# A two-layer hybrid trunk on one core: exponents and low parts as steps of their own, other PSUM banks for the token groups

## The chip, the cores and the metric

One core of a Trainium2 chip. The metric is the device time of one execution in microseconds; the time before is the median of three runs. All matrix work is in fp32 or in a split of fp32 in two parts, on TensorE (PE); the other engines are VectorE (DVE), ScalarE (ACT), GpSimd (POOL) and SyncE (SP), which issues the DMAs.

## What is computed

A trunk of two layers on 512 tokens of width 1024. The parts around the change are the attention with sinks and the retention of each layer:

```python
for l in range(DEPTH):
    h = rms_norm(x, norm_mix_g[l])
    aq, ak, av, rq, rk, rv, rg, sz, sxbc, sdt = jnp.split(h @ w_in[l], offs, axis=-1)
    ya = swa_sink_attention(aq, ak, av, attn_sinks[l], attn_bias)
    yr = retention(rq, rk, rv, rg, ret_gn_g[l])
    ys = ssd_mixer(sz, sxbc, sdt, ...)
    x = x + jnp.concatenate([ya, yr, ys], axis=-1) @ w_out[l]
    h = rms_norm(x, norm_ffn_g[l])
    x = x + conv_ffn(h, ffn_w_up[l], ...)
return rms_norm(x, final_norm_g)
# attention: chunks of 64 queries, 128 keys, 8 heads
p = softmax(concat([logits + bias, sink]))[..., :-1];  out = p @ v
# retention: q, k rotated; per head y normed by its mean and variance, scaled, times silu(g)
```

## The kernel before

**Split weights.** Every product of the dense parts is three matmuls of 128x512: w_hi with h_hi, w_hi with h_lo, and w_lo with h_hi. The weights stream through four slots. A pack is 128 by 512 (four tiles of 128x128): SP loads it into `w_raw` once POOL has made the low part of the pack before it in the slot, ScalarE copies it rounded into `w_hi` (L516) once PE has finished the run that used the slot (`run_done`), and POOL subtracts to get `w_lo` (L405). ScalarE makes packs where its own program says so: `hi_to(p)` makes all up to p, and each waits for its slot. A unit of eight tiles is 24 matmuls, of four tiles 12.

**The order.** All five engines follow one list of names by hand, `SCHEDULE` (L91), for the part of a layer up to the output projection. Each engine runs its own share of a step, in the order of the list, and passes over a step that has no share for it. A wait stands in the program of the engine that waits, so whatever comes later in the list on that engine stands behind it. The steps that matter here:

- `GQ0..3`, `GV0..3`: the first four packs of the token groups (retention's q and k; its v). PE works on all four blocks of 128 tokens at once, one PSUM bank for each token block, `token_banks`/`group_banks` = dense0, dense1, mix2, mix3 (L793, L1162). `LQ0..3`, `LV0..3`: the last four packs, one token block after the other. On DVE, `LQn` is the rotation and `LVn` the centring of a block (L1010 to L1012, evacuating the bank). On ScalarE, `LQ3` and `LV3` make four packs; `LV3` the ones for D20 and D21, whose slots LV3 itself frees.
- `ASn`: logits of two chunks on PE in banks mix0 and mix1, and transposed v in mix4; DVE adds the bias, takes the maximum and the sink's difference (L951 to L967); ScalarE copies the v window (L623) and takes the exponents, one of the sinks and eight of 128x128 (L626, L629).
- `AXn`: DVE divides by the sum (L971 to L974). `ATn`: PE transposes the probabilities into mix2 and mix3, ScalarE copies them (L634). `AVn`: PE's product with v, ScalarE's high part (L640), DVE's low part (L984).
- `Dn`: dense unit n, on bank n % 2; PE waits until unit n - 2 is evacuated, DVE evacuates (L836, or L827 for the output projection, D28 to D51, where x is added). D20 to D23 are the gate z of the SSD, D24 to D27 that of the retention; ScalarE applies silu to them (L564, L569).
- `ZMn`: DVE multiplies by silu(z) (L843), ScalarE squares (L610); after ZM1 and ZM3 POOL adds two squares (L437), and `SN0`, `SN1` sum over partitions on PE; ScalarE makes the factor, `SXn` scales (L937) and splits two tiles (L533 on ScalarE, L774 on DVE).
- `RXn`: retention's output tile, scaled and gated on DVE (L1049, L1051), high part on ScalarE, low part on DVE (L1054), which waits for ScalarE in between. D44 to D51 read these tiles, D44 waiting for each one as it comes to it.

SB, SA, RT, RA, RB and the like are steps of the SSD and of the retention that the change doesn't touch. After the list come the gated MLP's two halves: loops over 12 and 10 pairs of up units (`up(0)`, `up(1)`), each half followed by eight down units.

`unit()` (L1114) runs a unit. With `wait_for_tile` it waits, tile by tile, for the activations: D44 (`ret_tile`), the first down unit of each half (`g_tile`, L1463) and `up(0)` of the first half (`h_tile`, L1135, where the normed x of tile 7 comes last).

Of the kernel before, what the change touches and what calls it, by code (L numbers as in the profile page):

```python
# [19 lines left out]
D, S, P = 1024, 512, 128  # L20
# [5 lines left out]
NB = S // BLK  # L26
# [5 lines left out]
SLOTS = 4  # L32
# [6 lines left out]
GROUP = 4  # L39
# [18 lines left out]
def segments():  # L58
# [31 lines left out]

SCHEDULE = (  # L91
# [5 lines left out]
).split()  # L97


# [94 lines left out]
def build(nc, a, out):  # L194
    f32, f32r = mybir.dt.float32, mybir.dt.float32r
    ALU, ACT, AX = mybir.AluOpType, mybir.ActivationFunctionType, mybir.AxisListType
    with ExitStack() as ctx:
# [247 lines left out]
        def _(act):  # L445
# [60 lines left out]
            with act.Fori(0, DEPTH) as l:  # L506
# [28 lines left out]
                for name in SCHEDULE:  # L535
# [85 lines left out]
                    elif step == "AS":  # L621
                        act.wait_ge(m_ready[4], ready(name, 2, l))
                        nc.scalar.activation(vwin[:, n % 2, :, :], M[4][:, 0:2 * P].rearrange(  # L623
                            "p (c d) -> p c d", c=2), ACT.Copy).then_inc(m_free[4], 1)
                        act.wait_ge(lg_in, l * 4 + n + 1)
                        link(nc.scalar.activation(sk[:, :], sk[:, :], ACT.Exp))  # L626
                        for r in range(8):
# [80 lines left out]
        def _(dve):  # L708
# [58 lines left out]
            with dve.Fori(0, DEPTH) as l:  # L767
# [22 lines left out]
                            link(ins)  # L790
                    ins.then_inc(conv_summed, 1)

                token_banks = (dense[0], dense[1], M[2], M[3])  # L793
                V.memset(ak[:, 0:CH], 0.0)
                V.memset(av[:, 0:CH], 0.0)
                for name in SCHEDULE:
# [179 lines left out]
                    elif step == "AV":  # L976
                        av_bank = banks_of(name)[0]
                        for c in range(2):
# [3 lines left out]
                            if c == 0:  # L982
# [1 line left out]
                            V.tensor_tensor(m_lo[:, 4:8, at:at + CH], src,  # L984
                                            m_hi[:, 4:8, at:at + CH].bitcast(f32), ALU.subtract)\
                                .then_inc(m_free[av_bank] if c else a_lo, 1)
                    elif step == "LQ":
                        if n:
                            dve.wait_ge(rot_done, l * 4 + n)
                        dve.wait_ge(run_done, l * N_SEGS + (SEG0 + UNIT_END[U_RK + n]))  # L990
# [11 lines left out]
                                               ALU.mult, ALU.mult).then_inc(evac, 1)  # L1002
                        dve.wait_ge(evac, l * N_EV + U_RK + n + 1)
                        V.tensor_tensor(qk[:, n, :], qk[:, n, :], rot[:, :], ALU.add).then_inc(rot_done, 1)
                    elif step == "LV":
                        if n:
                            dve.wait_ge(evac, l * N_EV + U_RV + n)
                        dve.wait_ge(run_done, l * N_SEGS + (SEG0 + UNIT_END[U_RV + n]))
# [6 lines left out]
                    elif step == "RA":  # L1015
                        dec = consts["decin"][:, :].rearrange("p (t j s) -> p t j s", t=2, j=2)
                        for j in range(2):
                            dve.wait_ge(m_ready[1 + j], ready(name, j, l))
                            V.tensor_tensor(ar("rpt", 2, 2)[:, :, j, :], M[1 + j][:, 0:256].rearrange(
                                "p (t s) -> p t s", t=2), dec[:, :, j, :], ALU.mult).then_inc(m_free[1 + j], 1)  # L1020
                        V.tensor_tensor(kd.rearrange("p (h d) -> p h d", h=4),
                                        qk[:, n, 0:256].rearrange("p (h d) -> p h d", h=4),
                                        consts["kdec"][:, :].unsqueeze(2).broadcast_to([P, 4, 64]), ALU.mult)
                        V.tensor_tensor(qd, qkt[:, n % 2, 2:4, :],
                                        consts["qdec"][:, :].rearrange("p (t s) -> p t s", t=2),
                                        ALU.mult).then_inc(qd_done, 1)
                    elif step == "RB":
                        if n < NB - 1:
                            dve.wait_ge(m_ready[5], ready(name, 2, l))
                            if n == 0:  # L1030
                                V.tensor_copy(rst, M[5][:, 0:256].rearrange("p (t s) -> p t s", t=2))\
                                    .then_inc(m_free[5], 1)
                            else:
                                for t in range(2):
                                    ins = V.scalar_tensor_tensor(rst[:, t, :], rst[:, t, :],
                                                                 consts["gch"][:, t:t + 1],
                                                                 M[5][:, P * t:P * t + P], ALU.mult, ALU.add)
                                    if t == 0:
                                        link(ins)
                                ins.then_inc(m_free[5], 1)  # L1040
                    elif step == "RQ":
                        c = slice(BLK * n, BLK * n + BLK)
                        dve.wait_ge(r_sqh, l * NB + n + 1)
                        V.tensor_tensor(m_lo[:, 8:12, c], rsq[:, :, c], m_hi[:, 8:12, c].bitcast(f32),
                                        ALU.subtract).then_inc(r_sql, 1)
                    elif step == "RX":
                        dve.wait_ge(r_rs, l * 4 + n + 1)
                        dve.wait_ge(g_silu, l * 4 + n + 1)
                        link(V.scalar_tensor_tensor(ry[:, n, :], ry[:, n, :], par["gng"][:, bass.ds(l * 4 + n, 1)],  # L1049
                                                    rs4[n], ALU.mult, ALU.mult))  # L1050
                        V.tensor_tensor(ry[:, n, :], ry[:, n, :], sg[:, n, :], ALU.mult).then_inc(rn_done, 1)  # L1051
                        dve.wait_ge(r_hi, l * 4 + n + 1)
                        dve.wait_ge(rn_done, l * 4 + n + 1)
                        lo_from(m_lo[:, 8 + n, :], ry[:, n, :], m_hi[:, 8 + n, :], r_lo)  # L1054
# [47 lines left out]
        def _(pe):  # L1102
# [8 lines left out]
            mm(dense[1][0:8, 0:8], relw, relw).then_inc(run_done, SEG0)  # L1111
            pe.wait_ge(relt_ready, 1)

            def unit(bankno, number, runs, src_hi, src_lo, wait_for_tile=None):  # L1114

                pe.wait_ge(evac, number + 1)
                d = dense[bankno][:, :]
                last = runs[-1][3] + runs[-1][4] - 1
                for slot, pack, t0, k0, m in runs:
                    pe.wait_ge(hi_ready, pack + 1)  # L1120
                    for j in range(m):
                        w = w_hi[:, slot, P * (t0 + j):P * (t0 + j) + P]
# [30 lines left out]
            def take(name, i, l):  # L1153

                pe.wait_ge(m_free[banks_of(name)[i]], ready(name, i, l))

            with pe.Fori(0, DEPTH) as l:
                def dense_unit(n, src, wait_for_tile=None):
                    runs = [(p % SLOTS, l * N_PACKS + p, t0, k0, m) for p, t0, k0, m in SEGS[n]]
                    unit(n % 2, l * N_EV + n - 2, runs, *src, wait_for_tile)  # L1160

                group_banks = (dense[0], dense[1], M[2], M[3])  # L1162

                def group_mm(u, k, low, start=False, stop=False):
# [41 lines left out]
                def token_mm(t, k, low, start=False, stop=False):  # L1206

                    w = (w_lo if low else w_hi)[:, k % SLOTS, :]
                    c = slice(BLK * t, BLK * t + BLK)
                    d = group_banks[t][:, :]  # L1210
                    ins = mm(d, h_hi[:, k, c], w, start, stop)
                    return ins if low else mm(d, h_lo[:, k, c], w, False, False)

                def token_pack(u, k):

                    pe.wait_ge(hi_ready, l * N_PACKS + 2 * u + k + 1)
                    for t in range(NB):
                        if k == 0 and u == U_RK and t >= 2:
                            take("AT0", t - 2, l)
                        elif k == 0:  # L1220
                            pe.wait_ge(evac, l * N_EV + u + t + 1 - (2 if u == U_RK else GROUP))
                        token_mm(t, k, False, start=k == 0)
                    pe.wait_ge(lo_ready, l * N_PACKS + 2 * u + k + 1 + SLOTS)
                    for t in range(NB):
# [22 lines left out]
                for name in SCHEDULE:  # L1247
# [132 lines left out]
                    elif step == "AT":  # L1380
                        pe.wait_ge(p_done, l * 4 + n + 1)
                        if n == 0:
                            pe.wait_ge(evac, l * N_EV + U_RV + NB)
                        l4 = lg.rearrange("p (g c m k) -> p g c m k", g=2, c=2, m=2)
                        for c in range(2):
                            take(name, c, l)
# [246 lines left out]
```

## Time and profile before

| | us |
|---|---|
| median of three runs | 1294.49 (1293.77 to 1294.52) |
| profiled execution | 1293.96 |
| its span, first to last instruction | 1292.2 |
| PE busy | 1263.6 (98%) |
| DVE, ACT, POOL busy | 627.6, 580.9, 585.0 |
| mean granted TensorE clock | 0.996 of full |

How to read it: matmuls overlap, one of 128x512 lasts 0.39 us and the next starts 0.227 us behind it, so a time on PE is best read from start to start. The names are the kernel's tiles (`dense`, `mix` are PSUM; `arena` is a shared SBUF area that holds most mixer tiles). Layer 0 has its attention at 118 to 205 us, layer 1 at 753 to 840.

### The profile page before, as it was taken

The page shows a single profiled execution, that of the slowest core. Times are in us where ns is not written, and L with a number is a line of the kernel's source. Part 1 is how long each engine was busy: PE and PEld are TensorE (multiplying, and loading weights), DVE is VectorE, ACT ScalarE, POOL GpSimd, SP SyncE. Part 2 cuts the span into 40 slices and gives each one's busy share as a digit, 9 for nine tenths or more (in the row PEclk, how much of TensorE's full clock was granted, in tenths as well). Part 3 has the DMA queues.
Part 4 walks back from the last instruction along what each step waited for, and adds up shares of the span by engine and source line. Part 5 has one row for each costly group of instructions (what it writes and reads, how often), then busy time and mean ns, then how long its engine had stood idle before and what let it go on. Part 6 is the DMA issues. An engine that isn't in the chain of part 4 may idle for free.

```text
span 1292.2 us, 21140 instructions
## 1 busy us (share of the span) xinstructions
PE 1263.6 (98%) x6066; PEld 1025.8 (79%) x6066; DVE 627.6 (49%) x962; ACT 580.9 (45%) x966; POOL 585.0 (45%) x438
## 2 busy tenths in 40 slices
PE   8999899999999999999999999999999999999996
PEld 5887678788888888888878877787888888888885
DVE  5858565564544103332248686545754430133323
ACT  6443395555443224443345236854643432244433
POOL 4543333355444445554445333425354444455541
PEclk9999999999999999999999999999999999999998
DMA  6353222243333333333333622213233333333333
GB/s 213 104 149 89 66 66 66 65 115 98 96 94 95 98 98 92 97 96 98 99 83 84 171 66 82 73 51 99 74 114 97 97 98 98 90 97 97 97 94 111
DMA packets 77483, 124.89 MB, mean 97 GB/s; under 512 B 7752, under 2 KB 20456, under 8 KB 77416
## 3 DMA queue, kind: packets, MB, share of 16 engines
q1 hardware_dynamic: 77416, 124.03, 33.8%
q8 instruction: 38, 0.62, 0.2%
q14 instruction: 29, 0.24, 0.1%
HBM read 121.45 MB, written 2.55 MB: 96 GB/s over the span
## 4 chain that ended last, share of the span: by engine, by line
issue 39%; PE 34%; POOL 18%; ACT 3%; DVE 3%; POOLq 2%; DMA 0%; SPq 0%; DVEq 0%; ACTq 0%
PE dense L1106 32%; POOL w_lo L405 18%; PE mix L1106 2%; POOLq L404 1%; DVE h_lo L735 1%; POOLq L418 1%; DMA x<-in_xT 0%; ACT w_hi L516 0%; DVE arena L1097 0%; DVE arena L1049 0%; ACT m_hi L533 0%; ACT arena L629 0%; ACT h_hi L458 0%; DVE x L827 0%; DVE ssq L743 0%
## 5 line engine op out<-in xcount | busy, mean ns | idle before, releaser
L405 POOL TENSOR_TENSOR w_lo<-w_raw,w_hi 128x512 fp32r<-128x512 f32 x424 | 576.5, 1374 | 676.3 <-ACT w_hi L516 670.5
L1106 PE MATMUL dense<-h_hi,w_hi 128*128 128x512 f32 x992 | 391.3, 394 | 3.8 <-DVE h_lo L735 3.1
L1106 PE MATMUL dense<-h_lo,w_hi 128*128 128x512 f32 x992 | 387.0, 390 | 0.0
L516 ACT ACTIVATE w_hi<-w_raw 128x512 fp32r<-128x512 f32 x422 | 256.6, 626 | 285.0 <-PE dense L1106 227.9
L1106 PE MATMUL dense<-h_hi,w_lo 128*128 128x512 f32 x992 | 266.4, 390 | 0.0
L1106 PEld LDWEIGHTS dense<-h_hi,w_hi 128*128 128x128 f32 x992 | 186.6, 188 | 46.1 <-issue 6.6
L1106 PEld LDWEIGHTS dense<-h_hi,w_lo 128*128 128x128 f32 x992 | 186.4, 188 | 40.5 <-issue 1.7
L1106 PEld LDWEIGHTS dense<-h_lo,w_hi 128*128 128x128 f32 x992 | 186.7, 188 | 39.5 <-issue 1.4
L1106 PE MATMUL dense<-m_hi,w_hi 128*128 128x512 f32 x544 | 213.4, 392 | 1.3 <-DVE x L827 1.3
L1106 PE MATMUL dense<-m_lo,w_hi 128*128 128x512 f32 x544 | 212.0, 390 | 0.0
L1106 PE MATMUL dense<-m_hi,w_lo 128*128 128x512 f32 x544 | 146.8, 389 | 0.0
L1106 PEld LDWEIGHTS dense<-m_hi,w_hi 128*128 128x128 f32 x544 | 102.1, 188 | 24.2 <-DVE x L827 3.0
L1106 PEld LDWEIGHTS dense<-m_hi,w_lo 128*128 128x128 f32 x544 | 102.1, 188 | 21.3
L1106 PEld LDWEIGHTS dense<-m_lo,w_hi 128*128 128x128 f32 x544 | 102.2, 188 | 20.9
L1087 DVE TENSOR_TENSOR x<-dense,x 128x512 f32<-128x512 f32 x32 | 22.1, 692 | 191.4 <-PE dense L1106 191.4
L1065 DVE TENSOR_TENSOR arena<-dense,rstd 128x512 f32<-128x512 f32 x44 | 30.4, 692 | 87.1 <-PE dense L1106 87.1
L687 ACT ACTIVATE arena<-arena 128x512 f32<-128x512 f32 x44 | 27.8, 632 | 85.7 <-DVE arena L1072 85.7
L1075 DVE TENSOR_TENSOR arena<-dense,rstd 128x512 f32<-128x512 f32 x44 | 30.4, 691 | 71.4 <-PE dense L1106 71.4
L1068 DVE SCALAR_TENSOR_TENSOR arena<-arena,params 128x512 f32<-128x512 f32 x44 | 35.5, 807 | 59.8 <-ACT arena L682 59.8
L458 ACT ACTIVATE h_hi<-x,params 128x512 fp32r<-128x512 f32 x39 | 28.2, 723 | 71.1 <-DVE x L1087 59.6
L827 DVE TENSOR_TENSOR x<-dense,x 128x512 f32<-128x512 f32 x48 | 32.6, 687 | 54.3 <-PE dense L1106 54.3
L1106 PE MATMUL mix<-arena 64*128 64x128 f32 (+4 forms) x696 | 57.2, 301 | 1.6 <-ACT arena L634 1.6
(203 smaller groups left out, 1191.4 us busy)
## 6 DMA issues: line engine op xcount, KB each, us to landing
w_raw<-in_w SPq DMA_DIRECT2D x428, 256.0 KB, 2.6
arena<-cum_rows SPq DMA_DIRECT2D x8, 512.0 KB, 6.1
x<-in_xT SPq DMA_DIRECT2D x8, 256.0 KB, 5.7
out_y<-arena SPq DMA_DIRECT2D x8, 256.0 KB, 2.2
arena<-exp_rows SPq DMA_DIRECT2D x12, 128.0 KB, 6.5
consts<-in_consts SPq DMA_DIRECT2D x1, 839.0 KB, 7.6
rel_scratch<-arena SPq DMA_DIRECT2D x1, 382.0 KB
bias<-rel_scratch SPq DMA_DIRECT2D x8, 32.0 KB, 2.4
```

Of the source, the lines that this page charges most:

```text
L404: pool.wait_ge(hi_ready, pack + 1)
L405: nc.gpsimd.tensor_tensor(w_lo[:, s, :], w_raw[:, s, :], w_hi[:, s, :].bitcast(f32), ALU.subtract).then_inc(lo_ready, 1)
L418: with pool.Fori(g0, g1) as i:
L458: nc.scalar.activation(h_hi[:, o, :], x[:, o, :], ACT.Copy, scale=gcol(e, o)).then_inc(h_hi_ready, 1)
L516: nc.scalar.activation(w_hi[:, slot, :], w_raw[:, slot, :], ACT.Copy).then_inc(hi_ready, 1)
L687: nc.scalar.activation(fs, fy, ACT.Silu).then_inc(f_silu, 1)
L827: V.tensor_tensor(x[:, o, :], d[:, :], x[:, o, :], ALU.add).then_inc(evac, 1)
L1065: V.tensor_tensor(fpad[:, 2:2 + S], dense[0][:, :], rstd[:, :], ALU.mult).then_inc(evac, 1)
L1068: ins = V.scalar_tensor_tensor(fy, fpad[:, 1:1 + S], par["fconv"][:, bass.ds(fi * 4 + 1, 1)], fy, ALU.mult, ALU.add)
L1075: V.tensor_tensor(fb, dense[1][:, :], rstd[:, :], ALU.mult).then_inc(evac, 1)
L1087: V.tensor_tensor(x[:, o, :], dense[n % 2][:, :], x[:, o, :], ALU.add).then_inc(evac, 1)
L1106: return T.matmul(dst, lhsT, rhs, start=start, stop=stop)
```

## The change

The list is rewritten: `QE` and `VE` are now DVE's evacuations of the token groups, `AE` the exponents on ScalarE, `RL` the low part of RX on DVE. `LQ`, `LV`, `AS` and `RX` keep the rest. In the list, AE0 stands behind GV3 and SB3; AT0 and AS1 stand ahead of LV3, and VE3 behind AS1; AX1 stands ahead of AV0, and ZM0 behind D21; AT2 stands ahead of SX0 and ZM3; each RL stands one D step behind its RX. The token groups' first two blocks take mix2 and mix3, the last two dense0 and dense1, with the waits that follow from it. In units with `wait_for_tile`, the last run is made by `last_run`, which takes the low parts of the weights of all tiles but the last before it waits for the last tile.

```diff
@@ SCHEDULE
-    "GQ0 GQ1 GQ2 GQ3 SB1 SA2 LQ0 LQ1 LQ2 LQ3 SB2 SA3 GV0 GV1 AS0 GV2 GV3 SB3 AX0 LV0 LV1 LV2 LV3 AT0 AS1 "
-    "D20 AV0 AX1 ZM0 D21 ZM1 AT1 AS2 D22 AX2 AV1 SN0 ZM2 D23 SX0 ZM3 AT2 AS3 D24 AX3 AV2 SN1 D25 SX1 D26 AT3 D27 AV3 "
+    "GQ0 GQ1 GQ2 GQ3 SB1 SA2 LQ0 QE0 LQ1 QE1 LQ2 QE2 LQ3 QE3 SB2 SA3 GV0 GV1 AS0 GV2 GV3 SB3 AE0 AX0 "
+    "LV0 VE0 LV1 VE1 LV2 VE2 AT0 AS1 LV3 AE1 VE3 D20 AX1 AV0 D21 ZM0 ZM1 AT1 AS2 AE2 D22 AX2 AV1 SN0 ZM2 "
+    "D23 AT2 SX0 ZM3 AS3 AE3 D24 AX3 AV2 SN1 D25 SX1 D26 AT3 D27 AV3 "
...
-    "D35 RX0 D36 RX1 D37 D38 RX2 D39 RX3 D40 D41 D42 D43 D44 D45 D46 D47 D48 D49 D50 D51"
+    "D35 RX0 D36 RL0 RX1 D37 RL1 D38 RX2 D39 RL2 RX3 D40 RL3 D41 D42 D43 D44 D45 D46 D47 D48 D49 D50 D51"
@@ ScalarE, step AS
                             "p (c d) -> p c d", c=2), ACT.Copy).then_inc(m_free[4], 1)
+                    elif step == "AE":
                         act.wait_ge(lg_in, l * 4 + n + 1)
@@ VectorE
-                token_banks = (dense[0], dense[1], M[2], M[3])
+                token_banks = (M[2], M[3], dense[0], dense[1])
...
-                    elif step == "LQ":
+                    elif step == "QE":
...
-                    elif step == "LV":
+                    elif step == "VE":
...
                         V.tensor_tensor(ry[:, n, :], ry[:, n, :], sg[:, n, :], ALU.mult).then_inc(rn_done, 1)
+                    elif step == "RL":
                         dve.wait_ge(r_hi, l * 4 + n + 1)
@@ TensorE
+            def last_run(d, run, src_hi, src_lo, wait_for_tile):
+                slot, pack, t0, k0, m = run
+                pe.wait_ge(hi_ready, pack + 1)
+                hi = [w_hi[:, slot, P * (t0 + j):P * (t0 + j) + P] for j in range(m)]
+                lo = [w_lo[:, slot, P * (t0 + j):P * (t0 + j) + P] for j in range(m)]
+                for j in range(m - 1):
+                    wait_for_tile(k0 + j)
+                    mm(d, hi[j], src_hi(k0 + j), start=k0 + j == 0, stop=False)
+                    mm(d, hi[j], src_lo(k0 + j), start=False, stop=False)
+                pe.wait_ge(lo_ready, pack + 1 + SLOTS)
+                for j in range(m - 1):
+                    mm(d, lo[j], src_hi(k0 + j), start=False, stop=False)
+                wait_for_tile(k0 + m - 1)
+                mm(d, hi[-1], src_hi(k0 + m - 1), start=False, stop=False)
+                mm(d, lo[-1], src_hi(k0 + m - 1), start=False, stop=False)
+                mm(d, hi[-1], src_lo(k0 + m - 1), start=False, stop=True).then_inc(run_done, 1)
@@ unit()
                 for slot, pack, t0, k0, m in runs:
+                    if wait_for_tile is not None and k0 + m - 1 == last and m > 1:
+                        last_run(d, runs[-1], src_hi, src_lo, wait_for_tile)
+                        continue
@@ token_mm, token_pack
-                    d = group_banks[t][:, :]
+                    d = token_banks[t][:, :]
...
-                        if k == 0 and u == U_RK and t >= 2:
-                            take("AT0", t - 2, l)
+                        if k == 0 and u == U_RK and t < 2:
+                            take("AT0", t, l)
                         elif k == 0:
-                            pe.wait_ge(evac, l * N_EV + u + t + 1 - (2 if u == U_RK else GROUP))
+                            pe.wait_ge(evac, l * N_EV + u + t + 1 - GROUP)
@@ TensorE, step AT
                         if n == 0:
-                            pe.wait_ge(evac, l * N_EV + U_RV + NB)
+                            pe.wait_ge(evac, l * N_EV + U_RV + 2)
```

## Rows read from the trace of the kernel before

**Rows 1.** The page's busy us, share of the span and instructions, PE.
```profile
PE 1263.6 (98%) x6066; PEld 1025.8 (79%) x6066; DVE 627.6 (49%) x962; ACT 580.9 (45%) x966; POOL 585.0 (45%) x438
```
**Rows 2.** PE's waits in the whole span: line, releaser, us in total, times, longest.
```profile
PE mix L1390 <- DVE arena L1012: 4.2, 2, 2.1
...
PE mix L1106 <- ACT arena L634: 1.6, 2, 0.8
...
PE dense L1106 <- POOL w_lo L405: 1.3, 2, 0.7
...
PE dense L1106 <- DVE x L827: 1.3, 4, 0.4
```
**Rows 3.** Windows from start to start: length, each engine's busy us, PEclk, DMA.
```profile
98.78:101.61 2.83, 2.83 (x15) 2.35 (x14) 2.83 (x11) 0.00 (x0) 0.00 (x0) 1.00 0.56 161
126.53:131.04 4.51, 3.48 (x16) 2.12 (x13) 4.29 (x8) 2.05 (x6) 2.52 (x2) 1.00 0.10 15
139.22:141.48 2.26, 0.17 (x2) 0.01 (x1) 1.93 (x3) 0.78 (x2) 2.26 (x3) 1.00 0.38 82
141.48:145.39 3.91, 3.91 (x26) 3.46 (x27) 0.01 (x1) 1.19 (x2) 1.57 (x2) 0.56 0.71 212
157.67:158.59 0.92, 0.16 (x1) 0.00 (x0) 0.92 (x2) 0.00 (x0) 0.00 (x0) 1.00 0.00 0
158.59:160.90 2.31, 2.31 (x26) 2.02 (x27) 1.15 (x2) 1.72 (x4) 0.50 (x1) 1.00 0.04 7
181.83:182.78 0.95, 0.16 (x1) 0.00 (x0) 0.95 (x2) 0.95 (x3) 0.45 (x1) 1.00 0.14 54
244.96:250.95 5.99, 5.77 (x25) 4.43 (x24) 5.22 (x7) 1.68 (x3) 2.54 (x2) 1.00 0.17 44
253.67:259.83 6.16, 5.75 (x26) 4.43 (x24) 3.11 (x5) 2.72 (x5) 3.64 (x3) 1.00 0.29 85
267.00:272.44 5.44, 5.44 (x26) 4.50 (x25) 2.89 (x5) 3.79 (x8) 3.10 (x3) 1.00 0.32 80
284.31:290.27 5.96, 5.70 (x25) 4.43 (x24) 4.72 (x8) 3.16 (x4) 1.30 (x1) 1.00 0.35 88
776.82:779.12 2.30, 2.30 (x26) 2.02 (x27) 0.01 (x1) 1.09 (x2) 1.58 (x2) 1.00 0.63 181
```
**Rows 4.** Order in time, SB3 to VE0 and AX1's multiply: start, us, instruction.
```profile
124.91 1.69 PE L1106 MATMUL mix<-arena 128*64 128x128 f32 x32
...
125.09 2.45 ACT L629 ACTIVATE arena<-arena,nmx 128x128 f32<-128x128 f32 x8
...
127.44 1.14 ACT L516 ACTIVATE w_hi<-w_raw 128x512 fp32r<-128x512 f32 x2
...
128.13 2.52 POOL L405 TENSOR_TENSOR w_lo<-w_raw,w_hi 128x512 fp32r<-128x512 f32 x2 [4.66 <-ACT w_hi L516]
...
129.71 2.02 DVE L974 TENSOR_TENSOR arena<-arena,den 128x1024 f32<-128x1024 f32 x1
...
131.65 0.68 DVE L1010 TENSOR_REDUCE vmean<-dense 128x4 f32<-128x512 f32 x1
...
132.63 0.75 DVE L1012 SCALAR_TENSOR_TENSOR arena<-dense,rstdc,vmean 128x512 f32<-128x512 f32 x1
...
157.31 1.22 DVE L974 TENSOR_TENSOR arena<-arena,den 128x1024 f32<-128x1024 f32 x1
```
**Rows 5.** Order in time, the silu of D21, then AT2's copies, ZM's sum, SN1.
```profile
160.75 0.62 ACT L564 ACTIVATE pad<-pad 128x512 f32<-128x512 f32 x1
...
182.15 1.07 ACT L634 ACTIVATE arena<-mix 128x512 f32<-128x512 f32 x2
...
182.33 1.28 POOL L437 TENSOR_TENSOR sq<-sq 128x512 f32<-128x512 f32 x1 [2.73 <-ACT sq L610]
...
183.86 1.13 PE L1106 MATMUL mix<-sq,consts 128*128 128x512 f32 x2
```
**Rows 6.** Order in time, one low part in the up loop.
```profile
400.86 1.30 POOL L405 TENSOR_TENSOR w_lo<-w_raw,w_hi 128x512 fp32r<-128x512 f32 x1 [0.78 <-ACT w_hi L516]
```

More of the change, by code:

```diff
@@ L1160, in dense_unit @@
                     unit(n % 2, l * N_EV + n - 2, runs, *src, wait_for_tile)
+                token_banks = (M[2], M[3], dense[0], dense[1])
                 group_banks = (dense[0], dense[1], M[2], M[3])
```

## The prediction

> **What bounds the kernel now.** I read the page's busy shares first: TensorE (PE) is busy 98% of the span [rows 1], so only PE's gaps and slow stretches can pay. An unhindered unit of 24 matmuls of 128x512 takes 5.44 us, 0.227 each [rows 3], and the change adds and removes no matmul. What PE waits for is the second view [rows 2]: 4.2 us, once per layer, for VectorE's evacuation of the retention values (L1012), and 1.3 to 1.6 us each for ScalarE's copies of the probabilities (L634), POOL's low parts (L405) and the evacuation of x (L827). The third view is windows cut at instruction starts [rows 3]; a window less the same work unhindered is what its wait costs, the slow restart with it. The fourth is the order in time around the first softmax and around the second group norm [rows 4, 5].
>
> **The change, part by part, per layer.**
>
> *Exponents as a step AE, behind GV3.* Now ScalarE runs the eight exponents from 125.09 to 127.54 and only then converts the last two packs of the value group, though their slots are free when GV2 and GV3 end, the latter before SB3's start at 124.91 and the former one pack (12 x 0.227 = 2.7 us) sooner; POOL's low parts follow at 128.13 [rows 4], and PE stands in LV0 twice. LV0 takes 4.51 us [rows 3]; twelve matmuls behind mixer work take 2.83. With both conversions ahead (1.14 / 2 = 0.57 each, a low part 2.52 / 2 = 1.26) the last high part is there at 125.6 and the last low part at 127.0; LV0 starts at 126.53 and asks for the low parts from 128.4 on. Gain 4.51 - 2.83 = 1.68. Price: the exponents start behind the last conversion and end at 125.6 + 0.2 (the sinks') + 2.45 = 128.27, which is 0.73 later.
>
> *Token banks.* AT0 needs the two mixer banks. Now tokens 2 and 3 sit there and AT0 waits for all four evacuations: PE stands 2.26 us (139.22 to 141.48) [rows 3]. Then tokens 0 and 1 are there, AT0 and AS1 go ahead of LV3, and AT0 asks for VE1 at the end of LV2: 126.53 + 2.83 + 2 x 2.72 = 134.80. The vector side: the division AX0 now ends at 131.65, 4.11 us behind the exponents [rows 4]. Its last multiply took 2.02 us beside POOL's low parts (busy 128.13 to 130.65), and the same multiply 1.22 us at 157.31 [rows 4]. In the new order POOL has nothing from 127.0 until LV3, so I take 1.22: AX0 ends at 128.27 + 4.11 - 0.80 = 131.58, an evacuation takes 1.73 (131.65 to the end of L1012, 133.38), VE0 and VE1 end at 135.05. That is 0.25 behind PE; as the small add of that chain was slowed too, I take 0.2. Gain 2.26 - 0.2 = 2.06. With 2.02 instead, AT0 waits 1.05 and the gain is 1.2. The Trainium skill ("SBUF — State Buffer", section "SBUF: two separate sides") says the port pair that VectorE and GpSimd share is an exclusive lock, taken by a two-input vector instruction or a GpSimd one for its whole length; by that rule the multiply is short where POOL is idle, which gives the first price, while a machine on which the 2.02 had another cause would give the second, 1.7 us more for the kernel.
>
> *The clock.* In layer 0 the granted clock reads 0.56 (near 1.2 of 2.4 GHz) for 141.48 to 145.39, right behind that stand; AT0 with AS1 takes 3.91 us there and 2.31 for AT1 with AS2 at full clock. In layer 1 an equal stand is followed by 2.30 at clock 1.00 [rows 3]. So 1.60 us comes back, once, in layer 0. Bounds: 0, if another wait draws the clock down, and 1.6.
>
> *LV3 behind AS1.* LV3, 2.72 us, now covers AS1's vector work; its own evacuation VE3 stands behind AS1's vector part (like kinds of instructions as AX0, so at most its 4.1 us) and ends by 137.1 + 4.1 + 1.73 = 142.9. D21 alone waits for it, at about 146.6 (D20 from 140.1, 5.44, AV0 about 1.1); D20 waits for VE2 only. ScalarE's four conversions for D20 and D21 now queue behind AT0's two copies (1.07 [rows 5]) and AS1's window copy, whose PE work ends before LV3 starts; LV3 frees the first slot 0.7 later. Cost nothing. If that cover goes, D20 waits up to 0.6 for one conversion.
>
> *Division AX1 ahead of AV0's low part, ZM0 behind D21.* Now AX1's multiply ends at 157.31 + 1.22 = 158.53 and AT1, having stood 0.92 us, starts at 158.59 [rows 3, 4]. New: the exponents end at about 140.0 + 0.6 + 0.2 + 2.45 = 143.3, D20's evacuation by 146.3, AX1 takes at most 4.1 and is done by 150.4; D21 ends at 152.1. Gain 0.92. AV0's low part is asked for by D36 only.
>
> *AT2 ahead of SX0 and ZM3 on ScalarE.* AV2 stands 0.95 us for AT2's copies [rows 2, 3]. They now come before SX0's splits, so this wait goes. But SN1 follows AV2 directly and waits for POOL's sum of ZM2 and ZM3, ready at 183.61, with SN1 started at 183.86 [rows 5]: that chain runs silu of D23, SX0's high parts, their low parts on VectorE, ZM3, square, sum, and the copies, 1.07 us, are put in front of it. Against that ScalarE gets ahead: the silu of D21 ran 0.15 before D22's start (160.75 against 160.90), since ZM0's square stood before it; with ZM0 behind D21 it can run 1.4 before, and this stretch is ScalarE's queue throughout, so I carry 1.2 through. SN1 can start 1.2 - 1.07 = 0.13 sooner by the chain, plus 0.2 for the slack it had: gain 0.3. Bounds: 0.95 (chain covers nothing) and a loss of 0.8 (nothing of the 1.2 arrives).
>
> *RX split into RX and RL.* Now VectorE sits through ScalarE's split before each low part, x is evacuated late, and D39 and D42 wait. The pairs D38 with D39 and D41 with D42 take 5.99 and 6.16 us against 5.44 [rows 3]. New, each RX costs VectorE two instructions and RL one, with a unit's work between a split and its low part. At 0.75 for the scaled kind and 0.68 for a plain one [rows 4], four RX and RL and five evacuations are 4 x (0.75 + 0.68 + 0.68) + 5 x 0.68 = 11.8 us, in five units of PE, 13.6, and an evacuation has a whole unit before it is missed. Some of these run slower beside POOL, as the division's multiply did, so I keep half of the gain as a bound: 0.55 + 0.72 = 1.27, from 0.6. RL3 is done four units before D44's last tile.
>
> *last_run.* In the first up unit PE stands for the last tile's low part; 5.96 against 5.44 [rows 3]. Three low matmuls (0.68 us) now go ahead of that tile, more than the 0.52: gain 0.5. D44, the first down units and the other up(0) iterations show no such wait: 0. The wait for the packs' low parts moves 0.45 us earlier. The code issues as many instructions; no DMA is added or moved, SP's and POOL's queues keep their order.
>
> **The sum.** 1.68 + 2.06 + 0.92 + 0.3 + 1.27 + 0.5 = 6.73 per layer, 13.5 for two; with the clock's 1.6, 15.1 us. The profiled execution took 1293.96 (span 1292.2, 1.8 around it): 1278.9. The median of the three runs, 1294.49, is 0.5 above it: **1279.4**.
>
> **Rivals.**
> *A: AT0 still waits, for AX0.* Multiply at 2.02, or the later exponents pushing more. For: the margin is under 0.3. Against: POOL has no work then. 1.7 us of gain less, and if a remaining stand of over 2 us kept the clock low, 1.6 more: 1281 to 1283.
> *B: SN1 becomes the wait.* The copies stretch a chain that was ready 0.25 ahead of PE. For: ScalarE has little idle time there. Against: the earlier silu. 2 x (0.3 + 0.8) = 2.2 less: 1281.6. With A: 1283.5.
> *C: slower.* The wait for low parts, hoisted in last_run, passes 30 times (24 up units, 6 others). It decides if low parts arrive later than asked: to turn 15.1 us into a loss of 2.6 each pass must cost 0.59 us. Against: in the up loop a low part made at 400.86 to 402.16 [rows 6] is asked for at 409.5 in the new order, 7.3 us of slack. It would give 1297.
> *D: nothing moves*: the waits only change their names, each gain taken by the next wait in the same layer. It needs every cover above to be false. 1294.5.
>
> **Chances.** Forecast 0.72 (own range 1277.5 to 1281), A or B or both 0.24, C 0.02, D 0.02. Range: the forecast's, widened to A and B and to the clock's bound: 1276.8 to 1283.5. A measurement of this kernel tells apart about 0.2% (2.6 us). Faster 0.96, same 0.02, slower 0.02.
>
> **What would show it.** Right: LV0 near 2.8 us with no wait on L516 or L405; the wait on L1012 under 0.5; clock 1.00 through AT0; AT1 with no wait on L974; AV2 with none on L634, and SN1 with one on POOL L437 of 0.5 to 0.8; no waits on x (L827) at D39 and D42; the first up unit at 5.44. Wrong: a stand at AT0 over 1 us (A), SN1 later than 23 us behind D22's start (B), waits on POOL's low parts inside the up loop (C), or a new wait of D20 or D21.

## The result, and the profile after

The changed kernel takes 1279.45 us, the median of four runs (1279.37 to 1279.6), against 1294.13 for the kernel before in the same comparison (1292.02 to 1294.52). The ratio is 0.989, with a 95% interval of 0.9873 to 0.9907. The forecast was 1279.4. The profiled execution took 1279.5, with a span of 1277.6: 14.6 less than before.

That the total fits does not make every term right. The page first, where PE's share answers to [rows 1]:

```profile
PE 1257.4 (98%) x6066; PEld 1025.3 (80%) x6066; DVE 630.5 (49%) x962; ACT 581.9 (46%) x966; POOL 586.5 (46%) x438
```

PE's longest waits over the whole span (line, releaser, total, times, longest), which answer to [rows 2]. The changed kernel's lines lie lower in the file: L405 is now L406, L634 is L636, L827 is L829, L1012 is L1014, L1106 is L1109 and L1390 is L1415:

```profile
PE dense L1109 <- DMA arena<-in_rel: 3.4, 1, 3.4
PE dense L1109 <- DVE h_lo L737: 2.6, 1, 2.6
PE mix L1109 <- POOL sq L438: 2.6, 2, 1.3
```

All four waits of [rows 2] have gone. The first two belong to the kernel's start. One is new: 1.3 us per layer for POOL's sum of squares (L438), ahead of SN1.

Windows from start to start in layer 0, in the columns of [rows 3]. They are LV0; AT0 with AS1; AT1 with AS2; AV2 up to SN1; D38 with D39; D41 with D42; the first up unit:

```profile
126.25:129.10 2.85, 2.85 (x16) 2.36 (x13) 2.25 (x5) 1.69 (x6) 0.47 (x1) 1.00 0.59 170
134.54:136.79 2.25, 2.25 (x27) 1.96 (x27) 1.68 (x4) 1.09 (x2) 0.00 (x0) 1.00 0.00 0
151.80:154.05 2.25, 2.25 (x28) 1.96 (x26) 1.96 (x3) 1.86 (x3) 1.35 (x1) 1.00 0.47 117
175.06:177.43 2.37, 1.09 (x10) 0.50 (x9) 2.27 (x4) 2.09 (x3) 1.26 (x1) 1.00 0.00 0
238.55:243.99 5.44, 5.44 (x25) 4.51 (x24) 4.23 (x6) 1.68 (x3) 2.55 (x2) 1.00 0.16 48
246.71:252.17 5.46, 5.46 (x25) 4.50 (x24) 3.17 (x5) 2.72 (x5) 2.98 (x3) 1.00 0.26 62
276.65:282.10 5.45, 5.45 (x25) 4.50 (x24) 4.72 (x8) 3.16 (x4) 1.29 (x1) 1.00 0.33 96
```

The number behind the length is PE's busy time; it equals the length in every row but the fourth. There PE is busy 1.09 of 2.37 us. AV2 itself took 1.08 before, from 182.78 [rows 3] to 183.86 [rows 5], so SN1 now stands 1.29 (a stand is the time that PE waits ahead of a step).

The order in time (start, us, instruction) around the first softmax, from D21 to the exponents of AE2, from the silu of D23 to SN1, and layer 1's first product after its norm:

```profile
125.49 2.45 ACT L631 ACTIVATE arena<-arena,nmx 128x128 f32<-128x128 f32 x8
...
129.67 1.22 DVE L976 TENSOR_TENSOR arena<-arena,den 128x1024 f32<-128x1024 f32 x1
...
133.66 0.75 DVE L1014 SCALAR_TENSOR_TENSOR arena<-mix,rstdc,vmean 128x512 f32<-128x512 f32 x1
...
134.54 1.03 PE L1415 MATMUL mix<-consts,arena 128*128 128x128 f32 x8
...
152.60 2.37 DVE L845 TENSOR_TENSOR arena<-arena,pad 128x512 f32<-128x512 f32 x2
...
152.70 1.72 POOL L406 TENSOR_TENSOR w_lo<-w_raw,w_hi 128x512 fp32r<-128x512 f32 x1 [1.43 <-ACT w_hi L517]
...
152.72 0.63 ACT L565 ACTIVATE pad<-pad 128x512 f32<-128x512 f32 x1
...
154.90 1.27 DVE L953 SCALAR_TENSOR_TENSOR arena<-mix,bias 128x512 f32<-128x512 f32 x2
...
158.44 2.45 ACT L631 ACTIVATE arena<-arena,nmx 128x128 f32<-128x128 f32 x8
...
171.24 0.63 ACT L565 ACTIVATE pad<-pad 128x512 f32<-128x512 f32 x1
...
171.77 1.07 ACT L636 ACTIVATE arena<-mix 128x512 f32<-128x512 f32 x2
...
172.73 1.15 ACT L534 ACTIVATE m_hi<-arena 128x512 fp32r<-128x512 f32 x2
...
176.03 1.26 POOL L438 TENSOR_TENSOR sq<-sq 128x512 f32<-128x512 f32 x1 [3.69 <-ACT sq L611]
...
177.43 1.12 PE L1109 MATMUL mix<-sq,consts 128*128 128x512 f32 x2 [1.28 <-POOL sq L438]
...
652.67 1.92 PE L1109 MATMUL mix<-x,wdt_g 128*32 128x512 f32 x16
```

The division's multiply beside an idle POOL takes 1.22 (it was 2.02 [rows 4]). VE1 ends at 133.66 + 0.75 = 134.41, and AT0 starts at 134.54, when PE gets to it. The copies of AT2 (171.77) do stand ahead of SX0's high parts (172.73), and POOL's sum, the end of that chain, comes 1.29 after PE wants it.

Cutting both traces at the same instruction, the product with `wdt_g`, gives a second measure that run-to-run noise at the kernel's ends doesn't touch. From layer 0's to layer 1's it was 25.53 to 660.89 before, 635.36 us, and is 25.27 to 652.67 now, 627.40. So layer 0 gained 7.96, layer 1 gained 6.34 (from this cut to the last sum of squares 617.61 and 611.27), and the start 0.26, which sum to 14.56. Below, "the layer" is this length in layer 0; 627.40 is what it is held against.

### The profile page after: what moved, and what is told of

Its sections match the earlier page's. It is cut to its first block, busy times and chain, and to the rows that moved or that the text cites. A ratio compares the mean times of both kernels' runs of the same rounds, so it can differ in the third digit from the quotient of the medians.

```text
span 1277.6 us, 21142 instructions
## 1 busy us (share of the span) xinstructions
PE 1257.4 (98%) x6066; PEld 1025.3 (80%) x6066; DVE 630.5 (49%) x962; ACT 581.9 (46%) x966; POOL 586.5 (46%) x438
## 4 chain that ended last, share of the span: by engine, by line
PE 41%; issue 38%; POOL 18%; POOLq 2%; DVE 1%; ACT 1%; DMA 0%; SPq 0%; DVEq 0%; ACTq 0%
PE dense L1109 38%; POOL w_lo L406 18%; PE mix L1109 2%; POOLq L405 1%; POOLq L419 1%; DVE ssq L761 0%; DVE arena L1100 0%; DMA x<-in_xT 0%; DVE ssq L745 0%; ACT h_hi L459 0%; PE mix L1432 0%; POOL sq L438 0%; ACT L481 0%; ACT L478 0%; DVE ones_r L768 0%
## 5 line engine op out<-in xcount | busy, mean ns | idle before, releaser
L406 POOL TENSOR_TENSOR w_lo<-w_raw,w_hi 128x512 fp32r<-128x512 f32 x424 | 577.9, 1377 | 655.6 <-ACT w_hi L517 651.0
L1109 PE MATMUL dense<-h_hi,w_hi 128*128 128x512 f32 x992 | 390.7, 394 | 2.9 <-DVE h_lo L737 2.6
L1109 PE MATMUL dense<-h_lo,w_hi 128*128 128x512 f32 x992 | 386.7, 390 | 0.0
L1109 PE MATMUL dense<-h_hi,w_lo 128*128 128x512 f32 x992 | 270.1, 390 | 0.0
L1109 PEld LDWEIGHTS dense<-h_hi,w_hi 128*128 128x128 f32 x992 | 186.5, 188 | 44.2 <-issue 4.3
L1109 PEld LDWEIGHTS dense<-h_hi,w_lo 128*128 128x128 f32 x992 | 186.3, 188 | 40.5 <-issue 1.7
L1109 PEld LDWEIGHTS dense<-h_lo,w_hi 128*128 128x128 f32 x992 | 186.6, 188 | 39.6 <-issue 1.4
L1109 PE MATMUL dense<-m_hi,w_hi 128*128 128x512 f32 x544 | 212.9, 391 | 0.0
L1109 PE MATMUL dense<-m_lo,w_hi 128*128 128x512 f32 x544 | 211.8, 389 | 0.0
L1109 PE MATMUL dense<-m_hi,w_lo 128*128 128x512 f32 x544 | 147.7, 389 | 0.0
L1109 PEld LDWEIGHTS dense<-m_hi,w_hi 128*128 128x128 f32 x544 | 102.1, 188 | 21.3
L1109 PEld LDWEIGHTS dense<-m_hi,w_lo 128*128 128x128 f32 x544 | 102.1, 188 | 21.3
L1109 PEld LDWEIGHTS dense<-m_lo,w_hi 128*128 128x128 f32 x544 | 102.2, 188 | 21.0
L829 DVE TENSOR_TENSOR x<-dense,x 128x512 f32<-128x512 f32 x48 | 33.0, 688 | 56.5 <-PE dense L1109 56.3
L1109 PE MATMUL mix<-arena 64*128 64x128 f32 (+4 forms) x696 | 56.3, 297 | 0.0
```

What stands on the lines that cost most here:

```text
L406: nc.gpsimd.tensor_tensor(w_lo[:, s, :], w_raw[:, s, :], w_hi[:, s, :].bitcast(f32), ALU.subtract).then_inc(lo_ready, 1)
L829: V.tensor_tensor(x[:, o, :], d[:, :], x[:, o, :], ALU.add).then_inc(evac, 1)
L1109: return T.matmul(dst, lhsT, rhs, start=start, stop=stop)
```

## The experiments

Each is the changed kernel with one edit, unless two are named. The kernel before, run beside them, had medians of 1293.8 to 1293.9; the changed kernel was not timed again beside them. So where two medians differ by about 1 us or less, the layer's length has to show the same. Expectations stand as they were on record before the run.

**AT2 back behind ZM3.**

```diff
-    "D23 AT2 SX0 ZM3 AS3 AE3 D24 ...
+    "D23 SX0 ZM3 AT2 AS3 AE3 D24 ...
```

> The changed kernel with one part undone: AT2 behind SX0 and ZM3 again. Theory (the copies were put into the chain that SN1 waits for, so the move bought nothing): AV2 stands about 1 us for the copies again, and SN1 then starts with no stand, about 0.3 us sooner than now (1.28 us of stand on POOL L438 in each layer now); the kernel 0 to 0.6 us faster than the changed one, 1278.9 to 1279.5. Rival (the move is worth the 0.95 us stand it removed): about 0.9 per layer slower, 1281.3.

Measured: 1277.75 (1277.67 to 1277.96), ratio 0.9872 [0.9855, 0.9888], layer 626.52. This part of the change makes the kernel 1.7 us slower, where the prediction's term had it 0.6 faster (2 x 0.3). The time is 1.2 below the expected range, since AV2 stands half of the 1 us that was expected. The order in time of this kernel:

```profile
171.14 0.63 ACT L565 ACTIVATE pad<-pad 128x512 f32<-128x512 f32 x1
...
171.68 1.14 ACT L534 ACTIVATE m_hi<-arena 128x512 fp32r<-128x512 f32 x2
...
174.79 1.07 ACT L636 ACTIVATE arena<-mix 128x512 f32<-128x512 f32 x2
...
174.97 1.28 POOL L438 TENSOR_TENSOR sq<-sq 128x512 f32<-128x512 f32 x1 [2.72 <-ACT sq L611]
...
175.43 1.14 PE L1109 MATMUL mix<-arena 128*64 128x256 f32 x8 [0.39 <-ACT arena L636]
```

POOL's sum starts at 174.97 against 176.03, 1.06 sooner; 0.10 of this is the silu's, the rest comes of the copies (1.07), which are no longer in its way. SN1's stand is gone, and AV2 waits 0.39 for the copies. It starts 1.46 behind the start of D24's last four matmuls (173.97), against 0.99 in the changed kernel, so PE loses 0.47 here instead of the 1.29 at SN1.

**ZM0 back ahead of D21's silu.**

```diff
-    "... D20 AX1 AV0 D21 ZM0 ZM1 AT1 ...
+    "... D20 AX1 AV0 ZM0 D21 ZM1 AT1 ...
```

> The changed kernel with ZM0 ahead of D21 again (D20 AX1 AV0 ZM0 D21 ZM1). The prediction took ZM0's move to bring ScalarE's queue 1.2 us forward up to SN1; the changed kernel's trace shows only about 0.5. Theory: ZM0 ahead of D21 can run in VectorE's idle time while D21 is on PE, so that ZM1 comes sooner, and SN1's stand (1.28) gets no longer or even shorter by up to 0.7 per layer: 1278.0 to 1279.5. Rival (the prediction's): the move is worth about 1.2 to the chain, and undone SN1 stands up to 2.5: 1281.9.

Measured: 1278.65 (1278.53 to 1278.72), ratio 0.9885 [0.9869, 0.9902], layer 626.97. The theory held. Its order in time (the line at 154.01 is D22's start), and its wait at SN1:

```profile
149.34 0.69 DVE L845 TENSOR_TENSOR arena<-arena,pad 128x512 f32<-128x512 f32 x1
...
152.68 0.63 ACT L565 ACTIVATE pad<-pad 128x512 f32<-128x512 f32 x1
...
153.35 1.14 DVE L845 TENSOR_TENSOR arena<-arena,pad 128x512 f32<-128x512 f32 x1 [0.70 <-ACT pad L565]
...
154.01 0.48 PE L1109 MATMUL dense<-h_hi,w_hi 128*128 128x512 f32 x1
...
157.95 2.45 ACT L631 ACTIVATE arena<-arena,nmx 128x128 f32<-128x128 f32 x8
```

```profile
PE mix L1109 <- POOL sq L438: 1.7, 2, 0.8
```

One multiply runs early and alone in 0.69; the changed kernel runs both in a row beside POOL's low part, 2.37 for the two. AE2's exponents come at 157.95 instead of 158.44, and SN1's stand falls from 1.3 to 0.8. And the silu of D21 runs 154.01 - 152.68 = 1.33 ahead of D22 here, exactly as in the changed kernel (152.72 and 154.05). So moving ZM0, which was to let ScalarE get ahead, won nothing on ScalarE; it only put two multiplies in a row on VectorE, which costs 0.43 in the layer and 0.8 us for the kernel.

**Both of these together.** The edits are the two above.

> The changed kernel with AT2 behind ZM3 and ZM0 ahead of D21, the two orders of before that each made it faster when put back alone (1277.75 and 1278.65). Theory: AT2 behind ZM3 leaves AV2 a stand of 0.55 us for the copies, ScalarE's queue comes 0.45 sooner with ZM0 in VectorE's idle time, so AV2 stands 0.1 and SN1 not at all: 0.45 per layer below 1277.75, 1276.9. Rival (the two act on the same wait and the second buys nothing): 1277.7.

Measured: 1276.64 (1276.32 to 1276.91), ratio 0.9867 [0.985, 0.9883], layer 626.11. It beats both kernels. PE's only waits in its trace are both at the kernel's start; none of the mixers' is left:

```profile
PE dense L1109 <- DMA arena<-in_rel: 3.3, 1, 3.3
PE dense L1109 <- DVE h_lo L737: 2.6, 1, 2.6
```

The layer is 627.40 - 626.11 = 1.29 shorter, SN1's whole stand.

**ZM3 ahead of SX0, AT2 where the change put it.** This shortens the chain to SN1 from the other side.

```diff
-    "D23 AT2 SX0 ZM3 AS3 AE3 D24 ...
+    "D23 AT2 ZM3 SX0 AS3 AE3 D24 ...
```

> The changed kernel with ZM3 ahead of SX0 (D23 AT2 ZM3 SX0 AS3). Theory: SX0's two splits and two low parts leave the chain to POOL's sum (about 2 us of it), the sum is ready some 1.3 us before AV2 ends, SN1 stands for nothing; two layers of 1.28 us: 1276.9. Rival: ScalarE and VectorE are full there, so AS3, AX3 or SX1 come late instead and the stand only moves: 1278.5 to 1279.5.

Measured: 1280.52 (1280.16 to 1280.83), ratio 0.9892 [0.9876, 0.9909], layer 627.86. The forecast of 1276.9 missed. The rival beside it had the mechanism, a stand that only moves, but this time is 1.0 above its range too. Its waits on PE, and two lines in order of time:

```profile
PE dense L1109 <- ACT w_hi L517: 1.7, 2, 0.9
...
PE mix L1109 <- ACT arena L636: 0.7, 2, 0.3
```

```profile
173.80 1.63 POOL L438 TENSOR_TENSOR sq<-sq 128x512 f32<-128x512 f32 x1 [1.41 <-ACT sq L611]
...
174.32 2.27 DVE L776 TENSOR_TENSOR m_lo<-arena,m_hi 128x512 fp32r<-128x512 f32 x2
```

SN1 no longer waits, but SX0's low parts now run beside POOL's sum and take 2.27 for the two, and ScalarE's queue is late by D27: 0.9 us for a high part there and 0.3 at AV3. The wait was passed on.

**SN1 behind D25.**

```diff
-    "... D24 AX3 AV2 SN1 D25 SX1 D26 AT3 ...
+    "... D24 AX3 AV2 D25 SN1 SX1 D26 AT3 ...
```

> The changed kernel with SN1 behind D25 instead of behind AV2. Theory: PE has D25's 5.4 us to do while POOL's sum is made, SN1's stand of 1.28 goes, and the group norm comes 4 us later on ScalarE, which has little idle time there: as with ZM3 ahead of SX0, part of it returns as waits for conversions at D27 or for the copies at AV3 or for SX1's low parts at D28: 1277 to 1279.5. Rival (that queue has slack enough): 1276.8.

Measured: 1283.17 (1281.12 to 1285.27), ratio 0.9923 [0.9906, 0.9939], layer 628.55. A miss. Its wait, at AV3:

```profile
PE mix L1109 <- ACT arena L636: 4.7, 2, 2.3
```

I had counted what PE gains by taking a dense unit first. The scale factor, SX1's splits and, behind them, AT3's copies all stand behind SN1's sum, so they came later (the copies start at 195.60), and AV3 stood 2.3 us. That is beyond the range of 1277 to 1279.5, which allowed for a part of it.

**AX1 back behind AV0's low part.**

```diff
-    "... D20 AX1 AV0 D21 ZM0 ZM1 AT1 ...
+    "... D20 AV0 AX1 D21 ZM0 ZM1 AT1 ...
```

> The changed kernel with AX1 behind AV0's low part again (D20 AV0 AX1 D21), ZM0 left behind D21. Theory: VectorE waits about 3 us for ScalarE's high part (table load, silu, two splits) before it divides, AT1 stands 0.9 us per layer again: 1281.3. Rival (the stand before was ZM0's or another wait of PE, and AX1 is early enough now): no stand at AT1, 1279.5.

Measured: 1280.38 (1279.5 to 1281.05), ratio 0.9897 [0.988, 0.9913], layer 627.61. It lies between the theory (1281.3) and the rival (1279.5), and neither had the reason. Its waits in the mixers:

```profile
PE mix L1415 <- DVE arena L976: 1.8, 2, 0.9
...
PE mix L1109 <- POOL sq L438: 0.7, 2, 0.4
```

The stand of 0.9 at AT1 came back, yet the layer is only 0.2 longer (the median is 0.9 above, but in this profile the product with `wdt_g` came at 26.18 instead of 25.27, before any of the edit): the chain of VectorE and ScalarE behind it runs on, so PE comes later to a sum that is ready when it was, and SN1's stand falls from 1.3 to 0.4. The profiled execution (1280.82) is 1.3 above the changed kernel's: 0.9 of it lies ahead of the edit, and 0.4, two layers of 0.2, are the edit's. The silu of D21, with AX1 back and ZM0 left behind D21, starts at 154.35, 1.73 ahead of D22 (156.08).

**The same edit where SN1 doesn't wait,** with AT2 behind ZM3.

> The changed kernel with AT2 behind ZM3 and AX1 behind AV0's low part. With SN1's stand there, putting AX1 back cost only about 0.2 us per layer, as AT1's 1.05 of stand was taken off SN1's. Theory (one slack, shared): without SN1's stand only AV2's 0.55 is left to take it from, so AX1's place is now worth 1.05 - 0.55 = 0.5 per layer: 1278.7. Rival (AX1's place is worth little in itself, as VectorE catches up anyway): as u_at2, 1277.8 to 1278.1.

Measured: 1279.22 (1279.12 to 1280.13), ratio 0.9889 [0.9873, 0.9906], layer 627.18. AX1's place is worth 1279.22 - 1277.75 = 1.5 us here, 627.18 - 626.52 = 0.66 in the layer, against 0.2 in the layer above. The only wait beside those of the start:

```profile
PE mix L1415 <- DVE arena L976: 1.8, 2, 0.9
```

The mechanism is the one of the theory (one slack, shared), the size 0.5 us above its 1278.7. AT1's stand replaced AV2's (0.47 in the kernel without this edit), just as it took most of SN1's above. These gains lie one behind the other on the same slack and don't add.

**Exponents back ahead of the last conversions.**

```diff
-    "... GV0 GV1 AS0 GV2 GV3 SB3 AE0 AX0 "
+    "... GV0 GV1 AS0 AE0 GV2 GV3 SB3 AX0 "
```

> The changed kernel with AE0 back right behind AS0, ahead of the conversions of GV2 and GV3. Theory: LV0 takes 4.5 us again (waits on L517 and L406), AX0's multiply runs beside POOL's low parts and takes 2.0 us again, and since LV0 is later by 1.7, AT0 still has no stand: 3.4 us slower than the changed kernel, 1282.8. Rival (conversions were hidden by the later exponents' own price, AT0's wait for AX0): under 1.5 slower, below 1281.

Measured: 1282.9 (1282.37 to 1283.09), ratio 0.991 [0.9893, 0.9926], layer 629.12. As expected. PE's longest wait in LV0, then POOL and VectorE in order of time:

```profile
PE mix L1109 <- POOL w_lo L406: 1.3, 2, 0.7
```

```profile
128.04 2.52 POOL L406 TENSOR_TENSOR w_lo<-w_raw,w_hi 128x512 fp32r<-128x512 f32 x2 [4.66 <-ACT w_hi L517]
...
128.84 0.51 DVE L974 TENSOR_TENSOR den<-den,sk 128x8 f32<-128x8 f32 x1
...
129.62 2.02 DVE L976 TENSOR_TENSOR arena<-arena,den 128x1024 f32<-128x1024 f32 x1
```

The multiply takes 2.02 again, now that POOL works beside it, and the small add of 128x8 ahead of it 0.51, where the changed kernel has 0.17 (at 129.23). The two kernels differ in AE0's place alone.

**The old banks and the old place of LV3.** AT0 waits for all four evacuations again, and the waits of the token packs follow the banks as they did before; the steps' split stays.

```diff
-                token_banks = (M[2], M[3], dense[0], dense[1])
+                token_banks = (dense[0], dense[1], M[2], M[3])
...
-    "LV0 VE0 LV1 VE1 LV2 VE2 AT0 AS1 LV3 AE1 VE3 D20 ...
+    "LV0 VE0 LV1 VE1 LV2 VE2 LV3 VE3 AT0 AS1 AE1 D20 ...
...
-                            pe.wait_ge(evac, l * N_EV + U_RV + 2)
+                            pe.wait_ge(evac, l * N_EV + U_RV + NB)
```

> The changed kernel with the token banks as before (dense0, dense1, mix2, mix3), LV3 and VE3 ahead of AT0, and AT0 waiting for all four evacuations. Theory: AT0 stands 2.2 us in each layer (4.4 us), and where the stand is followed by a granted clock near half, as in layer 0 before, 1.6 more: 1283.9 without and 1285.5 with one such stretch. Rival (the banks matter little once AE0 is moved): under 2 us slower, below 1281.5.

Measured: 1286.18 (1285.31 to 1287.3), ratio 0.9935 [0.9918, 0.9952], layer 631.25. It is the dearest part, 6.7 us. Windows of the profiled run: the stand, then AT0 with AS1 and what follows in layer 0, and the same two in layer 1; the first column behind the engines is the granted clock:

```profile
137.05:139.31 2.26, 0.16 (x2) 0.01 (x1) 1.93 (x3) 0.78 (x2) 2.26 (x3) 1.00 0.38 84
139.31:142.41 3.10, 3.10 (x27) 2.71 (x27) 0.17 (x1) 1.09 (x2) 1.58 (x2) 0.72 0.71 198
142.41:144.00 1.59, 1.59 (x6) 1.30 (x5) 1.49 (x3) 0.39 (x1) 0.00 (x0) 0.50 0.47 155
770.56:773.46 2.90, 2.90 (x26) 2.51 (x27) 0.17 (x1) 1.08 (x2) 1.57 (x2) 0.77 0.72 192
773.46:776.00 2.54, 2.54 (x9) 2.07 (x8) 2.40 (x4) 0.39 (x1) 0.00 (x0) 0.59 0.35 116
```

Two stands of 2.26 are 4.5 us; the rest, 1.3 in the fastest run (1285.31) and 3.3 in the slowest (1287.3), goes with the clock: the layer is 631.25 - 627.40 = 3.85 longer, 2.26 and 1.6. The granted clock falls to 0.72 and 0.50 behind the stand in layer 0, and here in layer 1 too, so this execution (1287.0) has two such stretches, where the expectation's 1285.5 had one; the runs at 1285.31 and 1285.36 would fit one.

**RL right behind RX.**

```diff
-    "D35 RX0 D36 RL0 RX1 D37 RL1 D38 RX2 D39 RL2 RX3 D40 RL3 D41 ...
+    "D35 RX0 RL0 D36 RX1 RL1 D37 D38 RX2 RL2 D39 RX3 RL3 D40 D41 ...
```

> The changed kernel with each RL right behind its RX. Theory: D39 and D42 wait for x again, 0.55 and 0.72 us per layer: 2.5 slower, 1282.0. Rival (the waits came from POOL's contention with VectorE and not from the wait for ScalarE): under 1 slower.

Measured: 1282.19 (1281.9 to 1282.5), ratio 0.9912 [0.9896, 0.9929], layer 628.66, so 1.26 in the layer and 2.7 in all, as expected. Its wait:

```profile
PE dense L1109 <- DVE x L829: 1.3, 4, 0.5
```

**No special last run.**

```diff
-                    if wait_for_tile is not None and k0 + m - 1 == last and m > 1:
+                    if False:
```

> The changed kernel without last_run: every run takes its tiles in the order of before. Theory: only the first up unit of each layer waits for tile 7's low part, 0.5 us each: 1.0 slower, 1280.5. Rival (the hoisted wait for low parts costs in the up loop): the time falls below 1279.2.

Measured: 1280.61 (1280.22 to 1280.9), ratio 0.9901 [0.9885, 0.9918], layer 627.88; 1.2 us, 0.48 in the layer, as expected. Its wait, for tile 7 of the normed x:

```profile
PE dense L1109 <- DVE h_lo L737: 0.5, 2, 0.3
```

## Why the forecast held, and where it was wrong

*Exponents behind the conversions: right.* LV0 took 4.51 - 2.85 = 1.66 less, with 1.68 forecast, and undoing it cost 3.45 us, two times 1.66 and a little.

*Token banks: right, the residual was nil.* AT0 was to wait 0.2 for VE1; it waits 0. The gain is 2.26, not 2.06. VE1 ends 0.13 before AT0 starts, so the margin was thin as said. The exponents' delay was as forecast: counted from LV0's start (126.25, and 126.53 before) they ran 0.68 later, with 0.73 forecast. What the forecast had too long was the small add ahead of the multiply (L972, 0.50 before, beside POOL; now 0.17): it had noticed that this add was slowed and allowed 0.05 for it. The step that decided was the multiply at 1.22 where POOL is idle. The Trainium skill ("SBUF — State Buffer", section "SBUF: two separate sides") gives as a reason the exclusive lock on the port pair that VectorE and GpSimd share; the trace agrees, with 1.22 beside no POOL work and 2.02 beside it, for the same instruction in two kernels that differ in the order alone (the changed one and the one with the exponents back). Rival A fell with it.

*The clock: right.* AT0 with AS1 takes 2.25 at granted clock 1.00, against 3.91 at 0.56 [rows 3]. Layer 0 gained 7.96 and layer 1 gained 6.34: the difference is 1.62, with 1.60 forecast.

*LV3 as cover, AX1 ahead of AV0: right in the trace, but the latter's gain was not its own.* D20 and D21 wait for nothing, AT1 doesn't stand. The stand of 0.92 did go; of it only 0.2 per layer is left when one asks what the kernel would take without this move, for SN1 would have stood less.

*AT2 ahead of SX0 and ZM3: wrong, in size and in sign.* Two steps failed. The first is "with ZM0 behind D21 it can run 1.4 before". The silu of D21 did get 1.33 ahead of D22 (152.72 against 154.05), but not by this move: with ZM0 put back it is 1.33 ahead as well, and with AX1 put back and ZM0 left it is 1.73 ahead. So either of the two moves seems to be enough (both put back was not run), and ZM0's, beside AX1's, added nothing. The second is "I carry 1.2 through". This stretch is not ScalarE's queue throughout: D21's silu releases ZM0 and ZM1 on VectorE, which took 2.37 beside POOL's low part, and AS2's add (L953) waited behind them until 154.90. The exponents of AE2 started 4.39 behind D22 against 4.80 before, so 0.41 arrived of 1.2; with ZM0 put back it is 3.94, so 0.86 arrives. The line of the kernel before, with D22 at 160.90 [rows 3]:

```profile
165.70 2.45 ACT L629 ACTIVATE arena<-arena,nmx 128x128 f32<-128x128 f32 x8
```

The copies stood in the chain for 1.07, as forecast. SN1 follows D22's start by 177.43 - 154.05 = 23.38, against 183.86 - 160.90 = 22.96 before and 22.66 forecast. In the windows AV2's 0.95 is gained and SN1's 1.29 is lost: -0.34 per layer instead of +0.3. Rival B had this mechanism, and its lower bound was a loss of 0.8; I gave it too little of the chance, since both sides of its race were to be read in the trace, and one of them, VectorE, I had left out. The three runs on this place confirm it from three sides: AT2 back gives 1.7, ZM0 back 0.8, both 2.8, and no stand is left. In that last kernel AV2 doesn't stand either, with AT2 in its old place: a lead of ScalarE that neither ZM0's nor AT2's move gave has removed the 0.95.

*RX and RL, last_run: right.* 5.99 + 6.16 - 5.44 - 5.46 = 1.25 against 1.27, and 5.96 - 5.45 = 0.51 against 0.5. The run without each gave back 1.26 and 0.48 in the layer. No wait on low parts shows in the up loop, so rival C is out; D, by which the time stays, is out by the time itself.

*The sum.* 1.66 + 2.26 + 0.92 - 0.34 + 1.25 + 0.51 = 6.26 per layer, against 6.34 measured in layer 1; with 1.6 for the clock and 0.26 at the start it is 14.4, of 14.6. The forecast's 15.1 had 0.64 per layer too much at SN1 and 0.2 too little at AT0. The start's 0.26 was not foreseen; kernels whose start is the same reached this product at 24.64 to 26.18, so I don't put it down to the change. For the profiled execution the sum gave 1278.9 and it took 1279.5. The 0.5 by which the median of before lay above its profiled run was added to the forecast and covered most of that error by chance: the changed kernel's median lies at its profiled run, for its runs hardly spread (last section). One figure of the rivals was added up wrongly: B with A is 1281.6 + 1.7 = 1283.3, not 1283.5.

The parts measured by undoing one each are 3.45, 6.7, 0.9, -1.7, -0.8, 2.7 and 1.2, 12.5 in sum against 14.7 for the whole. Part of the missing 2.2 is AX1's, which hides behind SN1's stand. Another is AV2's stand of 0.95 per layer: it doesn't come back when AT2 and ZM0 are both put back, so some other move had removed it already, as above. Which one was not tried.

## What to carry to other kernels

When a step is moved ahead on one engine, list what it is put in front of and what its predecessor releases on the other engines: a lead of 1.3 us on ScalarE arrived only to a third, because VectorE had two multiplies to do in a row there, beside POOL. And ask whether the lead comes of the move it is put down to: here it was there without it. Waits that lie one behind the other in the same stretch share one slack, so their gains don't add: undo each part alone, and a part that the whole hides, here one that cost 1.7 us, shows. Before a consumer is moved back to spare its wait, ask what starts from its result: SN1 a unit later cost 3.7 us.

## What the runs showed of the hardware

**Behind a stand of a good 2 us the granted clock fell in some places and not in others.** It was 0.56 behind the stand of 2.26 in layer 0 of the kernel before and 1.00 behind the equal one in layer 1 [rows 3]; it fell behind both in the kernel with the old banks, and it was 1.00 for the 2.37 us behind AV3's stand in layer 0 of the kernel with SN1 behind D25. The times of such kernels spread, and their mean granted clock goes with them: the latter took 1281.12 at a mean clock of 0.997, 1283.05 and 1283.3 at 0.996, and 1285.27 at 0.994; the kernel before took, beside the experiments, between 1291.84 at 0.997 and 1295.95 at 0.994. The changed kernel's four runs lie within 0.23 us. If each step of some 2 us is one fall behind one of the two stands, this is in line with the 1.6 of the profiled one; that is argued and not shown, for only the profiled executions show where the clock fell. Not every spread is the clock's: the kernel with AX1 put back took 1279.5 to 1281.05, all four at 0.997.

**An instruction on VectorE with two inputs in SBUF takes longer beside POOL.** The 128x1024 multiply went from 1.22 to 2.02, and the two low parts of SX0 from 1.29 in the changed kernel (at 173.40) to 2.27 beside POOL's sum, 1.7 and 1.8 times as much. A small one can lose far more in proportion: one of 128x8 (L968, the sinks' difference) took 0.17 at 157.73 in the changed kernel and 1.22 at 139.83, amid POOL's low parts (138.48 to 143.54). With one input in PSUM no such cost shows here: the two adds of the bias (L953) took 1.29 beside an idle POOL (136.78) and 1.28 from 175.21, where POOL's sum (from 176.03) overlaps the second. POOL pays as well: its sum took 1.63 beside SX0's low parts against 1.26, and a low part 1.72 beside ZM0 and ZM1 against 1.30 [rows 6].
